# A fused encoder block: the RWKV-7 recurrence gets one more pipeline stage, and its preparation moves into one shared pair of banks

## The reference

```python
kk = kk / jnp.maximum(jnp.sqrt(jnp.sum(kk * kk, axis=-1, keepdims=True)), 1e-12)
k = k * (1.0 + (a - 1.0) * k_a)
xs = (r, decay, k, v, -kk, kk * a)      # each (tokens, heads, 64)

def step(state, inp):
    r_t, w_t, k_t, v_t, a_t, b_t = inp
    sa = jnp.einsum('bhvk,bhk->bhv', state, a_t)
    state = (state * w_t[:, :, None, :] + sa[..., None] * b_t[:, :, None, :]
             + v_t[..., None] * k_t[:, :, None, :])
    return state, jnp.einsum('bhvk,bhk->bhv', state, r_t)
```

## Time and profile before

| | |
|---|---|
| median of 3 runs | 3137.7 us (3137.1 to 3142.6) |
| profiled execution | 3137.99 us, span 3136.3 us |
| busy in the span | PE 2874.0 (92%), PEld 1679.9 (54%), DVE 1204.9 (38%), ACT 1001.3 (32%), POOL 651.5 (21%) |
| mean granted clock of PE | 0.968 |
| the recurrence | 1262 to 1827 us of the span |

### The profile page before, as it was taken

How to read it: one execution, slowest core, us unless ns; L and a number is a source line. 1 busy time by engine, 2 the same in 40 slices (tenths; PEclk the granted TensorE clock), 3 DMA queues, 4 the chain that set the end, 5 groups by cost and what they waited for, 6 DMA issues and landing times. The chain is left out here.

```text
span 3136.3 us, 75601 instructions
## 1 busy us (share of the span) xinstructions
PE 2874.0 (92%) x29606; PEld 1679.9 (54%) x29607; DVE 1204.9 (38%) x2076; ACT 1001.3 (32%) x2002; POOL 651.5 (21%) x859
## 2 busy tenths in 40 slices
PE   8999899999799899688788769995999999999998
PEld 3444344443466566577777735554555555555554
DVE  2323211111587787567666613333111111111111
ACT  1211100000466566455545423441222222222221
POOL 0000110000110110556556400001222222222222
PEclk9999999999799999899999979996999999999999
DMA  3212211110420210111111045522777786766773
GB/s 118 67 50 67 60 41 60 60 60 29 118 65 8 66 38 8 31 42 39 38 47 34 18 163 201 187 105 96 261 267 269 264 287 226 239 230 227 267 240 87
DMA packets 172526, 374.89 MB, mean 120 GB/s; under 512 B 27217, under 2 KB 108625, under 8 KB 153202
## 3 DMA queue, kind: packets, MB, share of 16 engines
q10 hardware_dynamic: 31088, 182.46, 14.9%
q1 hardware_dynamic: 128098, 146.24, 14.1%
q0 software_dynamic: 13120, 43.00, 6.6%
HBM read 298.79 MB, written 72.88 MB: 119 GB/s over the span
## 5 line engine op out<-in xcount | busy, mean ns | idle before, releaser
L2039 PE MATMUL gu_ps<-wg_,xT 128*64 128x384 f32 (+1 forms) x2592 | 574.7, 380 | 1.9 <-issue 1.9
L2040 PE MATMUL gu_ps<-wu_,xT 128*64 128x384 f32 (+1 forms) x2592 | 574.7, 380 | 0.0
L2039 PEld LDWEIGHTS gu_ps<-wg_,xT 128*64 128x64 f32 x2592 | 324.0, 137 | 280.8 <-issue 280.8
L388 PE MATMUL p_ps<-h_all,w_ch 128*128 128x512 f32 (+1 forms) x896 | 388.0, 596 | 10.0 <-DMA w_ch<-in_w_in 10.0
L310 PE MATMUL qkv_ps<-w_sb,hT 128*128 128x512 f32 x768 | 336.9, 595 | 1.4 <-DVE hT L282 1.4
L2040 PEld LDWEIGHTS gu_ps<-wu_,xT 128*64 128x64 f32 x2592 | 324.0, 137 | 0.0
L2059 PE MATMUL y_ps<-wd_,hT 128*64 128x512 f32 x648 | 295.4, 598 | 0.1
L2060 PE MATMUL y_ps<-wd_,hT 128*64 128x512 f32 x648 | 295.4, 598 | 0.0
L388 PEld LDWEIGHTS p_ps<-h_all,w_ch 128*128 128x128 f32 (+1 forms) x896 | 166.1, 186 | 231.4 <-issue 231.4
L662 DVE TENSOR_TENSOR_SCAN prod<-keep,prod 128x512 f32<-128x512 f32 x192 | 236.4, 1275 | 54.1 <-ACT keep L608 53.0
L1651 PE MATMUL o_ps<-wo_sb,mixT_t 128*128 128x512 f32 x512 | 228.8, 601 | 18.8 <-DMA wo_sb<-in_w_out 18.8
(11 more groups left out here) (302 smaller groups left out, 4498.7 us busy)
## 6 DMA issues: line engine op xcount, KB each, us to landing
wg_<-in_w_exp_gate ACTq DMA_DIRECT2D x29, 2048.0 KB
wu_<-in_w_exp_up ACTq DMA_DIRECT2D x29, 2048.0 KB
wd_<-in_w_exp_down ACTq DMA_DIRECT2D x29, 2048.0 KB, 18.8
x_t<-in_x SPq DMA_DIRECT2D x32, 512.0 KB, 4.8
pT<-shifted SPq DMA_DIRECT2D x13, 1024.0 KB, 3.9
rkv<-pT SPq DMA_DIRECT2D x48, 256.0 KB, 3.6
mixT_t<-mixT SPq DMA_DIRECT2D x16, 512.0 KB, 4.0
out<-x_t SPq DMA_DIRECT2D x16, 512.0 KB, 2.7
```

What stands on the lines that cost most here:

```text
L388: last = pe.matmul(p_ps[0:width, s, g, :], w[:, s, k, 0:width], h_all[:, k, g * GT:(g + 1) * GT], start=(k == 0), stop=(k == KT - 1))
L2039: pe.matmul(gu_ps[half][LO, 0:wide], xT[:, k, :], wg[s][:, k, cols], start=(k == 0), stop=(k == KT - 1))
L2040: last = pe.matmul(gu_ps[half][HI, 0:wide], xT[:, k, :], wu[s][:, k, cols], start=(k == 0), stop=(k == KT - 1))
```

## The change

The work on a step is spread over five passes in place of four. The pass is now counted by p: m = p + 1 is prepared, p is turned and scored, n = p - 1 goes through its levels, b = p - 2 through the state, t = p - 3 through the norm. The loop has 20 passes in place of 19. X and Y serve the levels alone. The turns and scores move to the pair of banks that was R and is now Q, which they share with the lora products, the key norm, the variance, the bonus and the gate, one after the other, with waits between them. The score products of both kinds and the turned tiles follow one another in Q, each behind the reader of the one before. Buffers that live a pass longer are one deeper (`AR`, `ends`, `bonus` 4; `tok_bk`, `tok_v`, `SB1`, `SB2`, `XX` 3; `ATl` 2). T level 0 no longer waits for `SB2_ready`. The orders of all engines are written anew; `rate(m + 1)` moves to the end of the pass in front, the three exponentials of `falls` stand together, and POOL makes `key_and_bonus` and `keys` ahead of `levels`. Nothing is computed otherwise than before.

```diff
-        X, Y, Z, R = [pb(n, [P, 2, 512]) for n in ("X_ps", "Y_ps", "Z_ps", "R_ps")]
+        X, Y, Z, Q = [pb(n, [P, 2, 512]) for n in ("X_ps", "Y_ps", "Z_ps", "Q_ps")]
...
+                    if m >= 1:
+                        pool.wait_ge(scores_done, 2 * m)
...
+                for p in range(-1, STEPS):
+                    m = p + 1
+                    if there(m):
+                        key_and_bonus(m)
+                        keys(m)
+                    if there(p):
+                        levels(p)
+                    if there(m):
+                        operands(m)
...
+                def falls(m):
+                    act.wait_ge(L_ready, m + 1)
+                    if m >= 1:
+                        act.wait_ge(operands_ready, m)
+                    act.activation(both(Dec), both(Lsum), ACT.Exp, scale=-EXP_HALF)
+                    act.activation(both(DecI), both(Lsum), ACT.Exp, scale=EXP_HALF)
+                    act.activation(both(DecP), both(Lprev), ACT.Exp, scale=-EXP_HALF).then_inc(exp_ready, 1)
...
+                def turn_bk(p, t):
+                    pe.wait_ge(operands_ready, p + 1)
+                    if there(p + 1):
+                        pe.wait_ge(ss_ready, p + 2)
+                        pe.wait_ge(a_ready, p + 2)
+                    elif t >= 1:
+                        pe.wait_ge(out_ready, t)
                     if there(t):
                         pe.wait_ge(lnvar_ready, t + 1)
...
+                def turn_v_and_first_level(p):
+                    pe.wait_ge(loaded[p % 3], landed(p, 3) * 3)
+                    pe.wait_ge(tok_bk_ready, p + 1)
...
+                def scores1(p):
+                    pe.wait_ge(tok_v_ready, 2 * p + 2)
+                    score(p, b_t).then_inc(scores_done, 1)
+
+                def scores2(p):
+                    pe.wait_ge(SB1_ready, p + 1)
+                    score(p, k_t).then_inc(scores_done, 1)
```

More of the change, by code:

```diff
@@ L885, in _ @@
                 load_gate(1)
[L886 to L895, removed]
+                for p in range(-1, STEPS + 3):
+                    t = p - 3
+                    if there(p + 3):
+                        load_lora(p + 3)
+                    if p >= 0 and there(p + 2):
+                        load_rkv(p + 2)
+                    if there(t):
+                        sp.wait_ge(out_ready, t + 1)
+                        sp.dma_start(mix_v[:, rec.pairs_of(t), rec.tokens(t)], outp[:, t % 2, :, :]).then_inc(stored[t % 2], 16)
+                    if t >= 0 and there(t + 2):
+                        load_gate(t + 2)
                 for s in range(2):
@@ L908, in key_and_bonus, with keys @@
                     pool.tensor_tensor(rk[:, m % 2, :, :], k2[:, :, :], rkv[:, m % 3, 0, :, :], ALU.mult).then_inc(rk_ready, 1)
[L910 to L926, removed]
+                def keys(m):
                     pool.wait_ge(root_ready, m + 1)
@@ L1027, in _ @@
                 decay(0)
-                for n in range(-1, STEPS + 2):
-                    m, b, t = n + 1, n - 1, n - 2
+                rate(0)
+                for p in range(-1, STEPS + 3):
+                    m, n, b, t = p + 1, p - 1, p - 2, p - 3
+                    if there(n):
+                        copy_T(n, 0)
                     if there(b):
                         copy_U(b, 0)
-                    if there(n):
-                        turned(n)
                     if there(m):
-                        rate(m)
+                        log_root(m)
+                    if there(t):
+                        log_variance(t)
                     if there(b):
                         copy_sa(b, 0)
[L1038 to L1048, removed]
                     act.drain()
@@ L1202, in _ @@
                     if there(n):
[L1203 to L1214 removed]
                         mask_T(n, 4)
+                    if there(p):
+                        weigh_bonus(p)
                     if there(t):
@@ L1219, in _ @@
                         grow(n, 4)
+                    if there(b):
+                        state(b, 3)
             @block.tensor
```

375 lines of the change are left out of this document (194 added, 181 removed).

## The result

The changed kernel takes 3178.05 us (median of 4 runs, 3176.92 to 3187.81) against 3137.4 us before: a ratio of 1.0136, 95% interval 1.0123 to 1.0149, 41 us slower. The forecast was 26 us slower. In the profiled executions the spans are 3175.1 and 3136.3 us.

A forecast was written before the change was run, and what follows sets the result against it. PE was taken as the busiest engine in a ring of levels, with in-order queues making it wait. Twelve passes of 34.5 us plus 176.5 us of head and tail gave 26 us more than 3137.7: 3164 us, range 3146 to 3186.

The forecast's parts named there:

- The pass: One full pass of the new recurrence: 24.3 us of PE work plus waits, 33.7 us; 34.5 taken with pauses.
- The fall of the clock: Rival: PE's longer waits lower its clock in a quarter of passes, 3205 us; chance 0.10 shared with the no-overlap rival.
- The norm beside POOL: Before X level 4: both norm pairs slowed beside POOL, 5.64 us, delay DVE's mask; PE idles 4.2 us.
- the wait before X level 1: First long wait of a pass: PE idles 2.05 us for mask and copy of T, queued behind other DVE and ACT work.
- a sign of being wrong: PE's longest wait in a pass standing elsewhere than before X level 4, where some 4 us was forecast.
- SA behind the sigmoids: End of the pass: ACT does the sigmoids of decay(m+1) before copying SA; PE idles 1.25 us.
- The rival without slow pairs: Norm pairs keep 0.87 us each, so X level 4 starts 3.05 us sooner: pass 30.4 us, total 3126; chance 0.14.
- POOL's ring in the full pass: POOL's work from turns to operands, 25.8 us, fits inside the pass, so the next step's turns don't wait for it.
- Head and tail: Partly filled passes at the recurrence's start and end, with one extra pass: 94.6 + 81.9 = 176.5 us.
- The pauses without a releaser: PE's "issue" pauses stay, some falling into the waits: 1.0 us a pass added in place of 1.44.
- Theory B: Rival account in the follow-up experiments: PE's pauses without a releaser and the extra pass are all of the loss.

The follow-up runs named there:

- e1: The changed kernel with norm_scale and norm_add moved on DVE from behind grow(n, 3) to behind grow(n, 1), where POOL is idle: 3155.9 us.
- e2: The changed kernel with norm_scale done twice in place, writing the same values, with a drain between the two: 3218.71 us.
- e6: The kernel before the change, with norm_add moved on DVE to right behind norm_scale, where POOL is idle: 3135.78 us against 3138.06.

## Why the prediction was right

The steps one by one:

- *The pass.* 33.7 us was laid out, 33.99 measured between two scans; with the pauses 34.5 and 35.2. Twelve times 0.7 is 8 of the 15 us that were missing. Mean less undisturbed pass is 1.2 us, where 0.8 to 1.0 had been put in. The sum held PE's work at 24.3 us, at a full clock. The fall of the clock stood among the rivals, as whole passes at 0.64; what came was milder, 0.96 over the full passes, and it is part of what is missing.
- *The norm beside POOL.* Right in its kind: the norm's place costs 22 us (e1), more of it costs more (e2), and the same slow pair, where the next instruction waits for PE anyway, costs next to nothing (e6). The size was off: the two pairs took 4.3 to 5.5 us and not 5.64, since `norm_scale` stands partly beside `levels` (pairs of 1.5 us) and partly beside `operands` (up to 3.1). And PE's wait was 1.96 us, not 4.2 (1.8 to 2.6 in the full passes): PE came to X level 4 some 2 us later than laid out (the mask was ready 29.1 us after the pass's start, laid out 28.9; PE was through output 2 at 27.2 and not at 24.75). X level 1 began 0.6 us later, and from there to the next from-state product it took 3.5 us in place of 2.3, because the clock was at its lower level then: in the pass before, at 1.00, the same piece took 2.3 us (1649.53 to 1651.85, against 1683.89 to 1687.41). That pass lost its time to pauses instead (1.5 us). So the wait was over-sized and the work under-sized by about as much; that they cancel, since the mask was ready when it was laid out, is luck in part. In three of the eleven full passes counted between scans the wait before X level 1 was even the longer one (2.06 against 1.79 us in the clearest), which the prediction had named as a sign of being wrong.
- *The wait before X level 1.* 2.05 laid out, 1.88 measured; mask and copy of T were both late, as said, and the scan took 1.88 and its subtract 1.67 us.
- *SA behind the sigmoids.* 1.25 laid out, 0.99 measured.
- *The rival without slow pairs.* Its 30.4 us should read 30.25 (33.7 less 3.05 and 0.4), which moves it by 2 us and changes nothing.
- *POOL's ring in the full pass.* It didn't set the pace: `operands` ended at 1706.4, the next turns began at 1712.9.
- *Head and tail.* 176.5 us laid out, 184 measured: this is the other 7.5. Counted as the layout counts, from T level 0, the head is 96.5 us (94.6 laid out) and the tail 89.3 (81.9). The last two outputs come 37.4 us after the one in front of them, where I had taken over the 29.4 of before. But 6.5 of these 8 us are only the mark: ACT's copy of y of the same pass stands 2.0 us ahead of that output before (1797.27) and 4.5 us behind it after (1829.9). From one copy of y to the last it is 22.1 and 23.5 us, so the chain itself is 1.4 us longer: SA is copied up to 3.6 us after U there, behind the Ln table load (2.1 before, behind the Exp table's), and PE's granted clock was 0.61 against 0.71. What the sum missed is mostly that the tail was put together from pieces measured between different marks. The timeline of ACT, before and after:

```profile
1795.31 0.58 ACT L981 COPY y_sb<-Z_ps 128x512 f32<-128x512 f32 x1 [3.29 <-DVE S_state L1112]
...
1817.37 0.58 ACT L981 COPY y_sb<-Z_ps 128x512 f32<-128x512 f32 x1 [2.36 <-DVE S_state L1109]
```

```profile
1834.48 0.58 ACT L989 COPY y_sb<-Z_ps 128x512 f32<-128x512 f32 x1 [1.97 <-DVE S_state L1124]
...
1857.97 0.58 ACT L989 COPY y_sb<-Z_ps 128x512 f32<-128x512 f32 x1 [2.36 <-DVE S_state L1121]
```

*The pauses without a releaser.* Theory B's first half is out by their sum alone: 34.2 us in the 13 full steps before, 19.8 in the 12 full passes after. No run varied them, but the DMA records of the traces say when they end. One queue carries instructions, here in the kernel before from 1340 to 1750 us (packets, MB, share of the DMA engines):

```profile
q8 instruction: 93, 1.52, 1.6%
```

That is a transfer of 16 KB every 4.4 us. In the twelve traces, between 1340 and 1750 us, there are 272 pauses of PE of more than 0.4 us without a releaser, leaving out one of 0.76 us before X level 0 that comes in every step of the kernel before; 267 of them end 1.15 to 1.65 us after such a transfer has landed. A moment taken at random does so in 11% of cases, and the waits with a releaser in 13%. So nearly all these pauses look like PE out of instructions until the next ones have come. That is a reading of the traces, and no experiment confirms it; what makes a transfer late, and the pause of 0.76 us, stay open.

Not tried: the same norm beside a POOL that works on other memory, so that the slowing was tied to POOL only by place and time.

## What to carry to other kernels

A deeper pipeline removes the wait between two stages and leaves the queues: before adding a stage, ask what stands in front of each short instruction that PE waits for, on each engine, and try that order first (here 12 us gained for three moved calls, against 41 lost for a stage with its first order). Count head and tail: a stage is paid in partly filled passes, here some 10 us net of 33, and they are slower than their share: PE's granted clock was 0.77 in the changed kernel's head and 0.61 in its last two passes. Place DVE work with two SBUF inputs by POOL's timetable, and where it must meet POOL, place it where nothing short is queued behind it.

## What the runs showed of the hardware

- DVE instructions whose tensors all lie in SBUF took longer beside POOL: two of 128x256 with two tensors 2.4 to 2.8 us in place of 0.88, a scan of 128x512 1.88 in place of 1.22, its subtract 1.67 in place of 0.69. Adds that read one input from PSUM kept their 0.69. That POOL is the cause is inferred from place and time.
- The same pair was slowed less beside POOL's 128x256 masks (1.5 us) than beside its 128x512 products (2.8).
- Two pieces of DVE work that each fit a gap of 1.9 us brought 22 and 5 us, each moved there alone (the 5 within noise), and together (with a third edit) 12: these gains didn't add.
- PE's granted clock fell to its lower level for 3.4 us at a time inside the recurrence (now and then 6.8), in the changed kernel several times right behind a wait of about 2 us. Over the full passes it was 0.97 before, 0.96 in the changed kernel, 0.99 in e1 and 0.91 in e2.
- PE's pauses without a releaser ended 1.15 to 1.65 us after a 16 KB transfer of the instruction queue had landed, in 267 of 272 cases.
